# A mixture-of-experts block on one core: moving VectorE's expert choice, its weight split and GpSimd's list scatters

## What is computed

```python
x = layer_norm(ALPHA * x + g1 * y, ln1_g, ln1_b)      # x1
h = layer_norm(x) * (1 + sc2) + sh2                   # h2
# moe(h):
scores = sigmoid(h @ w_router)                        # 64 experts in 8 groups
biased = scores + router_bias
grp_score = top_k(biased.reshape(t, 8, 8), 2)[0].sum(-1)
_, top_g = top_k(grp_score, 4)                        # 4 of 8 groups
_, idx = top_k(where(group chosen, biased, -inf), 8)  # 8 experts a token
w = scores[idx] / sum * 2.5
# tokens sorted by expert, in blocks of at most 128, each through its expert
y = (silu(xb @ w_gate[e]) * (xb @ w_up[e])) @ w_down[e]
routed = sum over a token's 8 experts of w * y
shared = (silu(h @ w_sh_gate) * (h @ w_sh_up)) @ w_sh_down
x = layer_norm(ALPHA * x + g2 * (routed + shared), ln2_g, ln2_b)
```

## Time and profile before

| | us |
|---|---|
| median of 3 timed runs | 1849.58 |
| lowest and highest of them | 1846.86, 1855.94 |
| the profiled execution's own time | 1866.22 |
| its span, first to last instruction | 1864.5 |
| TensorE busy | 1707.2 (92%) |
| VectorE, ScalarE, GpSimd busy | 925.0, 844.7, 771.6 |
| mean granted TensorE clock | 0.961 of full |
| DMA | 218 GB/s over the span |

### The profile page before, as it was taken

The page is one execution under the profiler, slowest core; times in us unless marked ns, Lnnn a source line. Parts: engine busy times, 40 slices in busy tenths (PEclk is TensorE's granted clock), DMA queues, the critical chain, the costliest instruction groups (busy, mean ns, idle before and its releaser), DMA issues.

```text
span 1864.5 us, 30719 instructions
## 1 busy us (share of the span) xinstructions
PE 1707.2 (92%) x8566; PEld 1335.3 (72%) x8567; DVE 925.0 (50%) x1432; ACT 844.7 (45%) x956; POOL 771.6 (41%) x452
## 2 busy tenths in 40 slices
PE   5899999999899777999999989999999989999845
PEld 1667678888455665888877878888878768888631
DVE  6522310157578853564464455334644654465529
ACT  0521012251033422675575667445765765567622
POOL 4520000400003553475456656535665556546530
PEclk9899999999999888999999999999999989999878
DMA  9505531022542443599799899966998899889786
GB/s 350 182 12 177 168 121 37 26 91 71 201 178 97 154 135 123 215 321 295 225 294 305 262 301 335 290 174 195 327 323 247 274 303 322 260 258 301 247 257 268
DMA packets 104719, 406.50 MB, mean 218 GB/s; under 512 B 17836, under 2 KB 36393, under 8 KB 76512
## 3 DMA queue, kind: packets, MB, share of 16 engines
q1 hardware_dynamic: 64656, 288.82, 41.8%
q0 software_dynamic: 37424, 107.59, 23.7%
q10 hardware_dynamic: 2592, 9.44, 1.7%
HBM read 339.94 MB, written 84.72 MB: 228 GB/s over the span
## 4 chain that ended last, share of the span: by engine, by line
PE 61%; DMA 16%; DVE 7%; issue 6%; ACT 5%; POOL 2%; SPq 1%; ACTq 1%; POOLq 0%; DVEq 0%
PE ps L843 32%; PE ps L1917 11%; DMA arena<-hx_dram,arena 6%; PE ps L898 4%; PE ps L2058 4%; DMA raw<-w_exp_up 3%; DMA acc_dram<-arena 3%; PE ps L1865 2%; DMA wvs_raw<-w_in 2%; POOL d_split L582 1%; ACT gu_split L640 1%; ACT d_split L645 1%; PE ps L2048 1%; PE ps L1890 1%; PE ps L875 1%
## 5 line engine op out<-in xcount | busy, mean ns | idle before, releaser
L843 PE MATMUL ps<-gu_split,xT 128*128 (+1 forms) x2712 | 641.4, 392 | 5.8 <-issue 5.7
L843 PEld LDWEIGHTS ps<-gu_split,xT 128*128 128x128 f32 x2712 | 511.9, 189 | 116.7 <-issue 10.0
L843 PE MATMUL ps<-d_split,hTe 128*128 (+1 forms) x1356 | 358.0, 415 | 33.1 <-ACT arena L721 33.1
L582 POOL TENSOR_TENSOR d_split<-raw,d_split (+1 forms) x65 | 299.5, 4608 | 201.1 <-ACT d_split L645 200.4
L974 DVE TENSOR_TENSOR gu_split<-raw,gu_split (+1 forms) x130 | 294.3, 2305 | 127.7 <-ACT gu_split L640 123.7
L843 PEld LDWEIGHTS ps<-d_split,hTe 128*128 128x128 f32 x1356 | 259.5, 198 | 88.6 <-issue 36.7
L640 ACT ACTIVATE gu_split<-raw (+1 forms) x130 | 241.4, 1908 | 63.1 <-SPq L484 36.5
L601 POOL DMA_INDIRECT arena<-hx_dram,arena x108 | 137.9, 1277 | 191.2 <-DVE arena L1144 159.0
L1138 DVE TENSOR_TENSOR arena<-ps,arena 128x256 f32<-128x256 f32 x113 | 70.5, 624 | 284.0 <-ACT arena L727 282.9
L610 POOL DMA_INDIRECT acc_dram<-arena x104 | 170.0, 1635 | 86.3 <-DVE arena L1149 56.1
L1917 PE MATMUL ps<-hT_split,w_split 128*128 128x512 f32 (+1 forms) x816 | 192.3, 394 | 3.7 <-DVE w_split L1599 3.7
(11 more groups left out here) (287 smaller groups left out, 1437.7 us busy)
## 6 DMA issues: line engine op xcount, KB each, us to landing
raw<-w_exp_gate SPq DMA_DIRECT2D x64, 1024.0 KB
raw<-w_exp_up SPq DMA_DIRECT2D x64, 1024.0 KB
raw<-w_exp_down SPq DMA_DIRECT2D x64, 1024.0 KB
arena<-w_ada SPq DMA_DIRECT2D x16, 1024.0 KB, 4.9
arena<-x_dram SPq DMA_DIRECT2D x18, 512.0 KB, 11.4
arena<-acc_dram SPq DMA_DIRECT2D x18, 512.0 KB, 11.5
arena<-w_ada SPq DMA_DIRECT2D x4, 2048.0 KB, 27.5
w_raw<-w_in SPq DMA_DIRECT2D x16, 512.0 KB, 4.9
```

The source lines that it names most:

```text
L582: tt(d_split(q, 1), raw_d(q), d_split(q, 0).bitcast(F32), ALU.subtract).then_inc(d_low, 1)
L843: last = mm(dst, lhs(a, j), rhs(b, j), start=(t == 0), stop=(t == len(terms) - 1))
```

## The change

Five moves and one new wait; no operation is added or dropped.

1. DVE: `choose(2)`, the choice for tiles 4 and 5, no longer stands ahead of `x1_sum(8)`. Its first half `choose_groups(2)` now follows `h2_norm(8)`, its second half `choose_experts(2)` follows shared step 0. So `x1_sum(8)` and the shared weights' `gate_up_low(0)` come ahead of both.
2. DVE: `place(2)` moves from behind shared step 0 to behind shared step 1.
3. PE: `rank(2)` moves from step 0 to step 1, behind `turn_h(0)`.
4. DVE: `gate_up_low(1)` moves from the end of step 7 into step 8, behind the copy of the lists, the first two `next_gather` and `gate(8)`.
5. GpSimd: before each tile's 8 scatters (but tile 0's) it waits until all scatters of the tiles before have landed.

```diff
@@ fill_lists (GpSimd) @@
                 for i in range(*RG[g]):
+                    if i:
+                        pool.wait_ge(list_out, 16 * TOPK * i)
                     for k in range(TOPK):
@@ phase3_pe @@
                 if b == 0:
                     transpose_h2(NT - 1)
-                    rank(2)
                 if b == 1:
                     route(NT - 1)
                     turn_x(b + 2, p, b + 2 - NT)
                     pe.wait_ge(logit_out, NT)
                 if b >= 1:
                     turn_h(b - 1, 1 - p)
+                if b == 1:
+                    rank(2)
@@ phase3_dve @@
-                if i in (3, 5, 7):
+                if i in (3, 5):
                     choose(i // 2 - 1)
@@
                 else:
                     h2_norm(NT - 1)
+                    choose_groups(2)
@@ shared_step @@
-                if b == NT - 2:
+                if b == NT - 1:
                     gate_up_low(1)
-                if b == NT - 1:
                     for j in range(2):
@@
                 if b == 0:
-                    place(2)
+                    choose_experts(2)
                     choose_groups(3)
                 if b == 1:
+                    place(2)
                     choose_experts(3)
```

## The result

The changed kernel takes **1870.56 us** (median of 7 runs, 1862.04 to 1873.77), the kernel before 1849.22 in the same comparison: ratio 1.0113, 95% interval 1.0092 to 1.0133. It is slower by 21 us, where 1854 and at most 1863 were forecast. The profiled execution is one of these seven, 1863.19, the second lowest, with a span of 1861.4.

A forecast was written before the change was run, and what follows sets the result against it. TensorE sets the pace in the expert loop, so the first routed `gate_up`'s start decides. +2.9 up to it and +1.6 for the late gather make +4.5 on the median 1849.6: 1854 us, range 1839 to 1863.

The forecast's parts named there:

- Part 2: DVE's moved choice and `place(2)`: scatters of tiles 4 and 5 start 2.3 us later, at 656.7 instead of 654.36.
- Part 3: GpSimd's scatters from tile 4 on: four pauses at 1.6 us each add 6.4 ahead of the list reads.
- slack at `lists()` and last landing: Ahead of `lists()` before the change: list chain ends at 710.0, just ahead of PE at 711.2.
- Part 4: `lists()` to first routed `gate_up`: 15.9 us instead of 20.5; 4.6 of the 7.8 us gather wait come back.
- Part 5: Weight load behind `gate_up_low(1)`: third block's gather, issued after it, lands later than PE asks, +1.6 us (0 to 3).
- rival C: Slower: pauses cost more than 1.6 us beside ACT's 512 KB writes; over 0.5% slower beyond 2.8 each; chance 0.14.
- Part 1: DVE in shared step 0: `x1_sum(8)` and `gate_up_low(0)` ahead of the choice bring `x_low(0)` and `h2_norm(8)` 7.5 us sooner.
- the list chain as the new bound: Scatters and list reads: lists there at 718.7, PE waiting for them since 706.4.
- hole 4: PE's 7.82 us wait up to 745.97, where `turn_x(9)` waits for the first gather; forecast to go.
- the absence of standstills from the timed runs: Two profiled stops of PE, ACT and DVE, together 20.3 us, taken as mostly not in the timed runs.
- rank(4) then waits: In step 4, PE's `rank(4)` waits some 1.8 us for DVE's `choose_experts(4)`.
- Rival B: Timed runs have the standstills too and pauses end them: -15.8, 1834 us (1842 if half the launches); chance 0.2.

The follow-up runs named there:

- second look: The kernel before, unchanged, profiled once more to see whether the standstills come back: 1852.62 us, no standstill.
- The split alone: The kernel before with only `gate_up_low(1)` moved from step 7 to step 8, behind `gate(8)` and `h_low(7)`: ratio 0.9999 (0.9983 to 1.0016).

## Why the prediction was wrong

Counted from the anchor, in profiles without standstills, in us:

| term | forecast | measured |
|---|---|---|
| before: `lists()` / first / second `gate_up` | 94.6 / 115.0 / 124.4 | 94.9 / 114.9 / 124.3 |
| later start of the scatters (Part 2) | +2.3 | +4.1 |
| four pauses (Part 3) | +6.4 | +13.9 |
| slack at `lists()` and last landing | -1.2 | -1.0 |
| `lists()` to first `gate_up` (Part 4) | -4.6 | -3.3 |
| first to second `gate_up` (Part 5) | +1.6 | +3.4 |
| sum at the second `gate_up` | +4.5 | +17.1 |

(The measured times before are those of the second look, the others those of the profile after. Slack, forecast: PE at 711.2 where the list chain ended at 710.0. Measured: the wait ahead of the list reads was 3.24 in the second look at the kernel before and 2.17 after.)

**The term that failed is Part 3's price of a pause**, 1.6 where 3.5 was measured; four of them make 7.5 of the 12.6 us between the two sums. Its bounds, 0.4 to 4.6, held the four values (2.9, 2.3, 4.6 and 4.1 over the 0.30 of issue; the third is at the bound), but the value taken, 1.6, rested on another kind of transfer, the 2.8 from issue to landing of a 512 KB write. Pauses that short exist (1.43 us of idle time in the kernel with twice as many). The ones on the chain of the changed kernel are 1.8 to 3.4 times as long as that. That is rival C, which had put the point of decision at 2.8 a pause; the mean was 3.5. It got 0.14 of the chance. It had the direction right and the reason wrong: the smaller writes of ACT left the pauses as long, and the longest came while the DMA engines were all but idle. In the four profiles with these pauses their sum is 15.1 (after), 17.9, 15.5 and, on chip D, 16.3, so they vary. The timed runs lost 21.3 where the traces show 17.1, which is just inside the interval of the comparison (17.0 to 24.6 us). The profiled execution's own time is 7 us below the timed median, but that is no sign of cheaper pauses: it was 5.9 ahead of the second look already at the anchor.

The Trainium skill (DMA: Bandwidth & Descriptors, "Anatomy of one DMA — SWDGE (gpsimd) path") gives about 2.0 us for such a DMA, most of it the write's receipt, and calls it about constant. The shortest case here, 0.95 + 1.43 = 2.4 from the last scatter's start to the end of its wait, is near it; 0.96 + 4.89 = 5.9 isn't, and the measurement decides. The Trainium skill's advice to wait late (the same page, "Rules for kernel authors") was the better guide than its figure: waiting one tile later cost nothing on chip E.

**Part 5** had the gather's wait about right (1.15 for 1.6) and missed another 2 us: the first routed `gate_up` itself takes 7.74 instead of 5.73. Part 4 had charged 1.5 for the clock and stopped at the first `gate_up`. It is not the wait of 20 us for the lists that does this. With the pauses alone PE waits 21.33 there and its clock is full at this place (first row); with the moves alone it waits 6.36, on chip E, and the `gate_up` is as slow (second row):

```profile
743.00:748.00 5.00, 5.00 (x23) 4.18 (x23) 1.29 (x2) 1.94 (x2) 1.72 (x2) 1.00 0.47 164
```

```profile
731.93 7.73 PE L843 MATMUL ps<-gu_split,xT 128*128 x24
```

What these two kernels with the moved split have in common is the stop of 3.15 us just ahead, at `turn_x(10)`, which waits for `x_low(9)` behind the moved split, and with which the clock fell a second time (0.51). So this is a price of Part 4's move and not of the pauses.

**Part 2**: the way from the end of `x_low(2)` to the last row of `place(2)` took 16.4, where busy times of 14.5 were added up. DVE is not idle in between. One of its rows, 0.28 long elsewhere, took 2.63 and ended with GpSimd's `down_low`:

```profile
640.01 2.63 DVE L1017 TENSOR_TENSOR arena<-arena 128x128 f32<-128x128 f32 x1
```

```profile
637.89 4.59 POOL L584 TENSOR_TENSOR d_split<-raw,d_split 128x2048 fp32r<-128x2048 f32 x1
```

In the moves alone on chip E it is another row beside the same operation, ahead of `x_low(2)`, 4.54 instead of 0.17. The start at 656.75 against 656.7 forecast hit by luck, since this execution was 1.7 ahead at the anchor.

**Right** were: Part 1 (`x_low(2)` ends 7.5 sooner against the anchor), the list chain as the new bound with PE idle ahead of `lists()`, hole 4 gone (`turn_x(9)` has no wait for its gather) with the split ending 13.8 behind `lists()` (13.9 forecast), the absence of standstills from the timed runs, and that rank(4) then waits (1.19). The split alone shows that Part 4's gain is given back whole.

**Rival B** had 0.2, and its first half is true on chips C and D: there the standstills are in the timed runs too, and with the pauses 3 us are lost to them instead of some 20. But its price of -15.8 had the pauses at 1.6 each; at their real price nothing is left (0.9989). One reason against it, that tiles 0 to 3 showed no standstill, still holds and is unexplained: they too come in rows of 16.

**What stays open**: why some comparisons had standstills and others not (the chip, or what surrounds it: no chip came twice); what PE, ACT and DVE share with GpSimd's scatters then; what makes one landing four times as long as another; and whether a break without a wait would do. The trace names only "issue" and "remote".

## What to carry to other kernels

Before adding a wait to an engine, follow what is queued behind it to the engine that sets the pace, and see how much slack there is at that end: here there was none, PE already waited 0.5 us, so nearly every microsecond of every pause counted, while the same pauses off that chain were free. Price a landing by the longest that a trace shows, not by the shortest, and wait for work that is a batch old rather than for the last. And when one profile disagrees with the timed runs by tens of microseconds, compare on more than one chip before judging a change that acts on just that: this one reads 1.011 on one and 0.999 on another.

## What was not expected of the hardware

- The same kernel takes 1850 us on three chips (and in the first comparison) and 1872 on two, by two standstills of 10 us in which PE, ACT and DVE get almost nothing issued while GpSimd scatters at its even pace of 1.26 us.
- The wait for scatters of 128 pieces of 8 bytes, the last one issued just before, is 1.43 us at one place and 6.02 at another of the same kernel. Making ACT's 512 KB writes eight times smaller did not shorten it, and during a wait of 4.89 the share of the DMA engines was 0.01.
- After the wait of some 20 us PE's granted clock came back to 1.00 and fell to 0.50 again within 20 us, with a stop of only 3.15: a `gate_up` took 7.74 instead of 5.73. Without that stop, behind a wait of 21.33, it took 5.72.
- A DVE operation on 128x128 numbers that takes 0.28 us took 2.63 beside GpSimd's subtraction on 128x2048 (637.89 to 642.48) and ended with it.
